# Six gate chunks computed as seven half-size products each, with their sums of x kept in DRAM

## The reference, cut to what matters

```python
y_a = (attn_a * silu(z_a)) @ w_pa          # 256 rows of w_pa
y_b = (attn_b * silu(z_b)) @ w_pb          # 512 rows of w_pb
merged = sigmoid(r_a + b_merge[:D]) * y_a + sigmoid(r_b + b_merge[D:]) * y_b
return rmsnorm(x + merged @ w_out)
```

## Time and profile before

| | us |
|---|---|
| median of 3 runs | 443.84 |
| the profiled execution | 443.48 |
| its span, first to last instruction | 441.7 |
| PE busy | 431.6 (98%) |
| VectorE, ScalarE, GpSimd busy | 212.8, 198.5, 176.3 |
| mean granted clock of PE | 0.998 |

### The profile page before, as it was taken

How to read it: one execution, slowest core, us unless ns; L and a number is a source line. 1 busy time by engine, 2 the same in 40 slices (tenths; PEclk the granted TensorE clock), 3 DMA queues, 4 the chain that set the end, 5 groups by cost and what they waited for, 6 DMA issues and landing times.

```text
span 441.7 us, 6258 instructions
## 1 busy us (share of the span) xinstructions
PE 431.6 (98%) x2377; PEld 374.5 (85%) x2377; DVE 212.8 (48%) x367; ACT 198.5 (45%) x401; POOL 176.3 (40%) x113
## 2 busy tenths in 40 slices
PE   7899999999999999999999999999999999999995
PEld 6789998899889988988888888888888888888885
DVE  3831244344435446757857664827025173083334
ACT  5743555335544464567555554533223543332111
POOL 4744442243243333646499543534355354200000
PEclk9999999999999999999999999999999999999999
DMA  8962234622452263024122022222222284210421
GB/s 284 286 192 96 96 96 83 159 96 95 91 150 97 96 168 110 25 96 143 49 95 96 0 73 96 96 72 96 95 71 96 95 261 156 113 66 0 149 90 47
DMA packets 40044, 48.31 MB, mean 109 GB/s; under 512 B 3768, under 2 KB 35536, under 8 KB 40016
## 3 DMA queue, kind: packets, MB, share of 16 engines
q1 hardware_dynamic: 37568, 47.72, 34.4%
q10 hardware_dynamic: 2448, 0.21, 0.4%
HBM read 39.48 MB, written 2.15 MB: 94 GB/s over the span
## 4 chain that ended last, share of the span: by engine, by line
PE 96%; DMA 2%; DVE 1%; ACT 1%; SPq 0%; issue 0%; DVEq 0%; ACTq 0%
PE ps L766 20%; PE ps L770 20%; PE ps L767 20%; PE ps L816 4%; PE ps L818 4%; PE ps L817 4%; PE ps L890 3%; PE ps L974 3%; PE ps L975 3%; PE ps L973 3%; PE ps L873 3%; PE ps L917 3%; PE ps L907 2%; DMA xs<-in_x 2%; PE ps L865 1%; PE ps L850 0%
## 5 line engine op out<-in xcount | busy, mean ns | idle before, releaser
L662 POOL TENSOR_TENSOR w_lo<-raw,w_hi 128x1024 fp32r<-128x1024 f32 (+1 forms) x59 | 138.1, 2342 | 175.4 <-ACT w_hi L990 175.4
L766 PE MATMUL ps<-hT_hi,w_hi 128*128 128x512 f32 x336 | 135.0, 402 | 1.1 <-DVE hT_lo L1241 1.1
L770 PE MATMUL ps<-hT_lo,w_hi 128*128 128x512 f32 x336 | 131.2, 390 | 0.0
L767 PE MATMUL ps<-hT_hi,w_lo 128*128 128x512 f32 x336 | 131.1, 390 | 0.0
L770 PEld LDWEIGHTS ps<-hT_lo,w_hi 128*128 128x128 f32 x336 | 63.1, 188 | 13.5
L766 PEld LDWEIGHTS ps<-hT_hi,w_hi 128*128 128x128 f32 x336 | 63.2, 188 | 11.2 <-issue 1.3
L767 PEld LDWEIGHTS ps<-hT_hi,w_lo 128*128 128x128 f32 x336 | 63.3, 188 | 9.9
L990 ACT CAST w_hi<-raw 128x1024 fp32r<-128x1024 f32 (+1 forms) x58 | 59.2, 1020 | 8.3 <-PE ps L770 5.4
L816 PE MATMUL ps<-w_hi,hT_hi 128*128 128x256 f32 x160 | 45.6, 285 | 0.0
L818 PE MATMUL ps<-w_lo,hT_hi 128*128 128x256 f32 x160 | 44.7, 279 | 0.0
L817 PE MATMUL ps<-w_hi,hT_lo 128*128 128x256 f32 x160 | 44.6, 279 | 0.0
(11 more groups left out here) (148 smaller groups left out, 665.6 us busy)
## 6 DMA issues: line engine op xcount, KB each, us to landing
raw<-in_w_in SPq DMA_DIRECT2D x25, 1024.0 KB, 4.9
KTs<-KTs SPq DMA_DIRECT2D x20, 256.0 KB, 3.4
raw<-in_w_out SPq DMA_DIRECT2D x4, 1024.0 KB, 4.8
xs<-in_x SPq DMA_DIRECT2D x4, 512.0 KB, 5.3
raw<-in_w_pb SPq DMA_DIRECT2D x4, 512.0 KB, 4.1
res<-in_x SPq DMA_DIRECT2D x4, 512.0 KB, 3.9
out<-weighted SPq DMA_DIRECT2D x8, 256.0 KB, 2.1
raw<-in_w_in SPq DMA_DIRECT2D x2, 512.0 KB, 8.9
```

What stands on the lines that cost most here:

```text
L662: nc.gpsimd.tensor_tensor(ring(w_lo, n, kt), src, ring(w_hi, n, kt).bitcast(F32), ALU.subtract).then_inc(lo_ready, 1)
L766: pe.matmul(out, wh, hh, start=(k == 0), stop=False)
L767: pe.matmul(out, wl, hh, start=False, stop=False)
L770: return pe.matmul(out, wh, hl, start=False, stop=(k == kts - 1))
```

## The change

The chunks `ra` and `rb` of columns 0 to 255 stay as they are, steps 36 to 39. The other six (`SEVEN`: two branches, three chunks) leave the loop. x^T (1024 x 512) is cut in four quarters of 512 depths by 256 positions, each weight chunk in four of 512 depths by 128 columns. Seven products of quarters or of sums of quarters give all four quarters of the result (the Winograd form of Strassen's scheme), where plain blocks take eight. Each product is 4 depth tiles x 3 matmuls, of 256 columns.

- The four sums of x are formed by VectorE in slots 2 to 6 (`fold`, `fold_low`), with the high halves by ScalarE (`fold_high`), in memory that is used later by the attention. SP writes them to DRAM (`store_fold`, 4 x 1 MB, behind the loads 7 to 10) and reads them back (`load_fold`) after the last scores and the last values.
- The four sums of each weight chunk are formed by VectorE in the PSUM banks 4 and 5 (`sum_begin`, `sum_third`, `sum_last`), from one quarter that ScalarE copies there. Their high halves are cast by ScalarE, their low halves (`sum_low`) by VectorE; GpSimd keeps the low halves of the three products whose weights are plain quarters.
- Each product goes to one of four banks (0, 1, 6, 7). VectorE's `combine` adds the products up to the gate quarters (7 additions of 256 columns for a chunk), ScalarE copies the first product and squashes the finished halves.
- The eight branch steps, in halves of 9 matmuls, stand between the chunks: y0, seven products, y1, seven products, ..., y5, seven products, y6, y7. They use banks 2 and 3, the last one 4 and 5, and `merge` works in place in PSUM. All low halves of w_out are made by GpSimd, w_out from depth tile 2 on is cast only after the last product.

The weights for operation o are made about six operations ahead (`AHEAD`) in eight half-size slots.

```diff
-for j in range(ND // 2):
-    CHUNKS += [("ra", C_RA + 256 * j), ("rb", C_RB + 256 * j), ("y", 256 * j)]
+CHUNKS += [("ra", C_RA), ("rb", C_RB)]
...
+SEVEN = [(b, c) for c in range(1, ND // 2) for b in range(2)]
+PARTS = [part for q in range(NSEV) for part in (("y", q), ("r", q))] + [("y", d) for d in range(NSEV, ND)]
...
+    if item[0] != "wo":
+        DUE[item] = OP_OF[item] - AHEAD + (item[0] == "r" and item[2] == 3)
+    elif item[1] < 2:
+        DUE[item] = DUE[SPLITS[m + 1]]
+    else:
+        DUE[item] = R_DONE + (item[1] - 2) // 2
...
+            def product(o):
...
+                else:
+                    pe.wait_ge(taken[(g - 4) % 7], (g - 4) // 7 + 1)
...
+                for k in range(4):
+                    pe.matmul(out, wh[:, k, :], hh[:, k, :], start=(k == 0), stop=False)
+                    pe.matmul(out, wh[:, k, :], hl[:, k, :], start=False, stop=False)
+                    last = pe.matmul(out, wl[:, k, :], hh[:, k, :], start=False, stop=(k == 3))
+                last.then_inc(consumed, 1)
...
+            def branches(o):
...
+                if half == 0:
+                    if d == 0:
...
+                    else:
+                        pe.wait_ge(mrg_lo_ready, d)
...
+            def squash(q, j):
...
+                act.wait_ge(c12_ready if j else c21_ready, q + 1)
+                nc.scalar.activation(gate(b, c, j), gate(b, c, j), ACT.Tanh, scale=0.5,
+                                     bias=hbias[:, 8 * b + 2 * c + j:8 * b + 2 * c + j + 1]).then_inc(gate_ready, 1)
...
-            def merge(n):
...
+            def merge(d):
...
+                    dve.wait_ge(gate_ready, 4 * c)
+                y = ps[:, ybank(d), :]
+                link(nc.vector.scalar_tensor_tensor(out=y, in0=ga, scalar=1.0, in1=y, op0=ALU.add, op1=ALU.mult))
...
+            def fold(n):
...
+                def add(a, b, op, count):
+
+                    nc.vector.tensor_tensor(out, a, b, op).then_inc(folded_full[n], 1)
+                    dve.wait_ge(folded_full[n], count)
+
+                if n == 0:
...
+                    add(hi[2], hi[3], ALU.add, 1)
+                    add(out, lo[2], ALU.add, 2)
+                    add(out, lo[3], ALU.add, 3)
...
+            def fold_low(n):
+
+                hi, lo = (folded_early[:, n, e, :, :] for e in range(2))
+                dve.wait_ge(folded_hi[n], 1)
+                nc.vector.tensor_tensor(lo, fold_full(n), hi.bitcast(F32), ALU.subtract).then_inc(folded_lo[n], 1)
```

More of the change, by code:

```diff
@@ L131, in last_user @@
 def last_user(n):
-    return max([m for m in range(n) if m % 2 == n % 2 and step_kind(m) != "y"], default=None)
+    return n - 2 if n >= 2 else None
 def in_residues(n):
@@ L148, in taken_count @@
     return sum(1 for m in range(n + 1)
-               if m % 2 == n % 2 and step_kind(m) != "y" and not stacks(m) and not in_residues(m))
-def ysteps(n):
-    return sum(1 for m in range(n) if step_kind(m) == "y")
+               if m % 2 == n % 2 and not stacks(m) and not in_residues(m))
 def fills(kind):
@@ L473, in raw_waits, with splits_before @@
             for m in range(n % NRAW, n + 1, NRAW):
-                k, c = LOADS[m]
-                count += 0 if m == 0 else 32 if k == "w" and CHUNKS[c][0] == "y" else 16
+                count += 0 if m == 0 else 32 if LOADS[m][0] == "y" else 16
             return raw_in[n % NRAW], count
-        def halves_before(n):
-            return (2 * sum(1 for k, _ in LOADS[:n + 1] if k == "w"),
-                    2 * sum(1 for k, _ in LOADS[:n + 1] if k == "out"))
+        def splits_before(n):
+            return sum({"w": 2, "r": 7, "y": 2, "out": 2}[k] for k, _ in LOADS[:n + 1])
@@ L729, in _ @@
                     add_residue_groups()
+            for item in SPLITS:
+                if item not in VLOWS:
+                    split_low(item)
         @block.tensor
@@ L783, in start @@
                         weights_wait(n // 2 * 2 + 1)
[L784 to L793, removed]
+                    if last_user(n) is not None:
                         proj_taken_wait(pe, last_user(n))
@@ L948, in _ @@
+            for o, op in enumerate(OPS):
+                (product if op[0] == "r" else branches)(o)
             for i in range(TT):
@@ new lines, in prepare @@
+            def prepare(o):
+                for q in range(NSEV):
+                    at = o - first_due(q)
+                    if at == -1:
+                        sum_begin(q)
+                    elif at == 2:
+                        sum_low(q, 1)
+                    elif at == 3:
+                        sum_low(q, 2)
+                        sum_third(q)
+                    elif at == 4:
+                        sum_last(q)
+                    elif at == 5:
+                        sum_low(q, 3)
+                    elif at == 6:
+                        sum_low(q, 5)
```

476 lines of the change are left out of this document (368 added, 108 removed).

## The result

| | median, us (lowest to highest, runs) |
|---|---|
| before | 443.75 (443.39 to 444.29, 4) |
| after | 454.87 (452.77 to 459.0, 4) |
| ratio | 1.026, interval 1.019 to 1.034 |

A forecast was written before the change was run, and what follows sets the result against it. PE, busy 431.6 of 441.7 us, was taken to bound the kernel. 443.48 - 6.4 + 3.3 + 4.9 = 445.3, with 0.36 for the median of the runs 445.6 us; range 442.3 to 449.6.

The forecast's parts named there:

- PE's work: Gate products on PE: 288 products of 512 columns (65.3 us) become 504 of 256 (58.9 us), a gain of 6.4 us.
- the prediction's own signs of being wrong: No idle at 55, a seven-product period above 14.2 us, or products of 256 columns further apart than 0.117 us.
- The seven-product stretch: Two half branch steps and seven products, 13.9 us a period: VectorE, 85% busy, keeps up, so 0 us.
- Rival 4: VectorE's queue bounds the seven-product stretch: at 1 us a period, 6 us more, 451.6 us; chance 0.15.
- The sums of x: Slots 2 to 6: VectorE's additions and GpSimd's low halves exclude each other, the first head's mask comes late: 3.3 us.
- my walk: VectorE's sums and GpSimd's low halves followed in turn from 27.8 us, putting the first head's mask at 56.8 to 57.4.
- The end of the branch steps: Before the last branch step y7, PE waits for the merged low half of y6: 4.9 us.
- Rival 1, the clock: PE's clock falls to 1.2 GHz in the wait before y7, losing 2 us more: 447.6 us; chance 0.20.
- Transfers: 4 MB of sums stored behind loads 7 to 10 and read back 38 us before the first product: 0 us.
- The SBUF rule: VectorE with two SBUF inputs and GpSimd share one port pair as an exclusive lock: 3.3 us for the sums of x.

The follow-up runs named there:

- a3_both: After, with y7 waiting for y5's merged low half instead of y6's, and the first w_out load moved behind the sixth chunk's: 441.53 us, ratio 0.996.
- a4_sums_from_psum: a3_both with one operand of each sum of x and of its low half taken from PSUM instead of SBUF: 440.09 us, ratio 0.993.
- b1: Before, with one added wait: the last branch step starts only after the merged low half of the branch step ahead of it: 449.19 us, ratio 1.012.
- a1: After, with the last branch step y7 waiting for the merged low half of y5 instead of y6: 446.85 us, ratio 1.007.
- c1: a3_both with the last of the four sums of x formed in step 7 and its low half in step 8: 438.73 us, ratio 0.990.
- a2_w_out_load_behind: After, with the first load of w_out moved behind the load of the sixth gate chunk: 450.72 us, ratio 1.015.
- c2_last_sum_in_step_9: a3_both with the last of the four sums of x formed in step 9 and its low half in step 10: 439.75 us, ratio 0.992.

## Why the prediction was wrong

The measured 454.87 us lies outside the range of 442.3 to 449.6. By the prediction's own steps:

- **PE's work, -6.4.** Measured -4.8 (504 x 0.120 = 60.5 against 65.3); in a3_both, where PE doesn't wait there, the stretch with these products is 4.7 shorter than in before. The sign and the reading were right, the size was a third too large: I took the value step as the nearest row, as it has the same columns. The output product's 256-column part in before was as near: its last 48 products, up to the earlier trace rows, start 0.1198 apart. Had I read two rows of that form and not one, the term would have had 4.8 as its low bound. Products further apart than 0.117 us were also one of the prediction's own signs of being wrong.
- **The seven-product stretch, 0.** Right in the first four periods, which have no idle. Rival 4 did not come. VectorE and ScalarE kept up.
- **The sums of x, +3.3.** The mechanism was right and a4_sums_from_psum shows it; the size was 1.8, that is 1.25 for the scores and 0.5 for the turns. Counted from the first value product, my walk had the mask at 56.8 - 36.44 = 20.4 us, and it came at 56.37 - 37.29 = 19.1, 1.3 earlier. At the end of the third sum the walk was already 1.1 late (49.7 and 0.85 for the prologue, against 44.83 + 4.62). The walk took the plain sum of durations for each stretch of additions with a low half of GpSimd inside, and three of them were each 0.2 to 0.3 shorter: 5.83 and 5.87 us instead of 6.06, 4.56 instead of 4.84. The other 0.6 wasn't taken apart.
- **The end of the branch steps, +4.9.** Measured 5.1: the wait, its cause and its length held, step by step.
- **Rival 1, the clock.** This is the step that failed in judgement. I had the row that told it, and gave it 0.20, because it was one sample, and added that it might hold in some executions only. Each profile with such a wait shows it, and of b1's four runs even the fastest, 448.63, lies above the 447.3 that the wait alone would give. In the profiled execution it cost 2.7 (2 was the rival's figure) behind y7's wait and 1.6 behind the other. By the rule cited from the Trainium skill ("TensorE: Matmul & The Clock Gate", "Part 1: The HAM clock gate"), idle time brings the half rate: these windows agree, 0.50 after 3.2, 3.7 and 5.1 us of idle.
- **Transfers, 0.** This is the step that failed outright, 4.8 us. I costed the 8 MB of the sums and did not ask what else the change does to the transfers: it rewrites `LOADS`, and in a ring of three slots one more entry changes which buffer each later load waits for. The difference was in one line of the change, `LOADS += [("out", 0)] if part == ("y", NSEV - 1) else []`, which the excerpt shown ahead of the prediction leaves out. A walk of the ring for the last two chunks would have shown the sixth chunk's load behind the fifth's last low half. That load took 5.0 us (360.92 to 365.95), and PE's products in hand lasted until 363.8. It put PE 3.2 us idle, and 1.6 more at the lower clock.
- **What no step had.** +0.85 in the prologue and +1.2 behind the last product. The first varies: the first value product starts between 35.70 and 37.40 in kernels with the same prologue, and in the profiled after the clock stood at 0.72 and 0.50 between 12 and 16 us. The second is told below.

Sum with the measured terms: -4.8 + 1.8 + 5.1 + 2.7 + 3.2 + 1.6 + 0.4 + 0.85 + 1.2 = 12.05, against 12.0 between the spans. By these terms a1 should give back 7.8, and gave 8.0; a3 12.6, and gave 13.3; c1 1.8 more, and gave, by ratio to before, 0.996 - 0.990 of 443, that is 2.6, with 1.1 of the end in it. The terms 0.4, 0.85 and 1.2 were only read.

The SBUF rule cited in the prediction (the Trainium skill, "SBUF — State Buffer", "SBUF: two separate sides") was tested here by its converse: with one operand in PSUM the additions keep their 1.22 beside GpSimd.

## What to carry to other kernels

The waits of 3.2 to 6.5 us on the otherwise full TensorE here cost themselves and a third to a half as much again, since the work behind them ran at 1.2 GHz for a while; so a step that ends in front of a chain of other engines should have unrelated work put between, or only wait for what it overwrites. When a change touches the list of loads of a ring, walk the ring: one load inserted early ties the later ones to other releases. And a saving in columns is to be multiplied by the slowest rate that rows of that shape show, not by one of them.

## What was not expected of the hardware

- The clock's price behind an idle PE, with the lower level each time: idle 3.2 us, 1.6 lost; 3.7 us, 1.7 lost; 5.1 us, 2.7 lost; 6.5 us (a2_w_out_load_behind), 398.85 - 392.46 - 4.08 = 2.3 lost. In the first two the clock was still at full speed when PE began again, and fell while it worked (0.97 in the window 366 to 368, 0.50 in the next). The idles of at most 2.4 us in the prologue go with a clock of 1.00 in some profiled executions and with 0.50 for a while in others.
- Products of 256 columns with a new stationary tile each time stand 0.120 us apart in gate steps, seven products and output product, and 0.1168 to 0.118 in value steps, in up to 102 in a row; for half the columns this is 53% and 51 to 52% of the 0.227 of 512.
- The end of the program. In seven profiled kernels, among them after, the span ends 6.6 to 6.8 us behind the last product's start, in six others, among them before, 5.6 us. In the last 7 us of after one packet of an instruction queue is moved, as in the other six of the seven and in none of the six (queue, packets, MB, share of the DMA engines):

```profile
q14 instruction: 1, 0.01, 0.3%
```

c1_last_sum_in_step_7 differs from c2_last_sum_in_step_9 only in the place of two VectorE additions, one low half and their cast; c1 is without the packet and ends at 5.6 us, c2 has it and ends at 6.65. So the packet and the 1.1 us go together, and that the one makes the other is only argued.
